# First norm, bias rows, cumulative-sum rows and the entry of the down stages: four edits to a two-block transformer kernel on one core

## The reference

```python
# first block
h = rms_norm(x, ln_mix_pre)
proj = h @ w_in                      # q, k, v, z, xbc, dt_raw
attn = moba_attention(q, k, v, rel_bias)   # one block of 256: causal, with a relative bias per head
ssm  = mamba2_mixer(z, xbc, dt_raw, ...)   # 16 heads, chunks of 128 tokens
#   a_cs = cumsum(dt * a);  seg = a_cs[l] - a_cs[s];  decay = exp(causal(seg))
#   y_diag = (C B^T * decay) @ (x * dt)
x = x + rms_norm(concat(attn, ssm) @ w_out, ln_mix_post)
h = rms_norm(x, ln_ffn_pre)
u = causal_conv(h @ w_ffn_up);  f = (gelu(gate) * up) @ w_ffn_down
x = x + rms_norm(f, ln_ffn_post)
# second block: rwkv7 in both directions + grouped attention, w_out2, and a
# product-key expert layer (top 16 of 128x128 experts in 8 heads), then a last norm
```

## Time and profile before

| | |
|---|---|
| median of 3 runs | 3450.74 us (3445.03 to 3453.64) |
| the profiled execution | 3449.55 us; span of its trace 3447.8 us |
| PE busy in the span | 3327.2 us (97%) |
| DVE, ACT, POOL busy | 2564.5 us (74%), 1609.3 us (47%), 131.9 us (4%) |
| w_in stage (chunks 0 to 44) | from 16 us to about 340 us |
| share of the DMA engines, 30 to 340 us | 0.47 |

### The profile page before, as it was taken

How to read it: one execution, slowest core, us unless ns; L and a number is a source line. 1 busy time by engine, 2 the same in 40 slices (tenths; PEclk the granted TensorE clock), 3 DMA queues, 4 the chain that set the end, 5 groups by cost and what they waited for, 6 DMA issues and landing times.

```text
span 3447.8 us, 68503 instructions
## 1 busy us (share of the span) xinstructions
PE 3327.2 (97%) x24846; PEld 2959.5 (86%) x24846; DVE 2564.5 (74%) x4463; ACT 1609.3 (47%) x2555; POOL 131.9 (4%) x143
## 2 busy tenths in 40 slices
PE   8999999999999999988888999999999999999998
PEld 6888878888888777777777899899999999999998
DVE  6766587776868788776665688877777887777776
ACT  5445554444444555543334522454544545454543
POOL 0000000000000000000000001100001010101000
PEclk9999999999999999999999999999999999999999
DMA  5534545555555544430002545688878788878764
GB/s 194 176 136 163 188 144 177 192 171 191 183 191 184 192 132 141 140 111 9 9 15 86 179 158 175 242 278 282 280 268 286 282 319 265 299 255 304 251 230 158
DMA packets 176239, 658.33 MB, mean 191 GB/s; under 512 B 20080, under 2 KB 28400, under 8 KB 167408
## 3 DMA queue, kind: packets, MB, share of 16 engines
q1 hardware_dynamic: 159744, 559.15, 48.1%
q0 software_dynamic: 16336, 97.03, 7.7%
HBM read 637.99 MB, written 17.04 MB: 190 GB/s over the span
## 4 chain that ended last, share of the span: by engine, by line
PE 82%; DVE 9%; DMA 3%; ACT 3%; issue 2%; ACTq 0%; DVEq 0%; SPq 0%
PE bank L609 47%; PE bank L611 23%; PE bank L1002 5%; DMA raw<-in_v_tab 3%; DVE w_lo L2113 2%; PE bank L1305 2%; DVE hot_row L3088 1%; ACT w_hi L1390 1%; DVE hot_col L3083 1%; DVE proj L2730 1%; PE bank L973 0%; DVE h_tok L3114 0%; PE bank L947 0%; PE bank L1013 0%; DMA gates<-g_stage 0%
## 5 line engine op out<-in xcount | busy, mean ns | idle before, releaser
L609 PE MATMUL bank<-h_two,w_hi 128*128 128x512 f32 (+1 forms) x5360 | 1821.9, 390 | 26.9 <-DVE w_lo L2113 19.2
L611 PE MATMUL bank<-h_two,w_lo 128*128 128x256 f32 (+1 forms) x5360 | 1466.8, 274 | 0.0
L2113 DVE TENSOR_TENSOR w_lo<-raw,w_hi 128x1024 fp32r<-128x1024 f32 (+1 forms) x1054 | 1228.5, 1184 | 232.8 <-ACT w_hi L1390 230.9
L1390 ACT ACTIVATE w_hi<-raw 128x1024 fp32r<-128x1024 f32 (+1 forms) x1054 | 1044.6, 1024 | 459.7 <-PE bank L611 239.9
L609 PEld LDWEIGHTS bank<-h_two,w_hi 128*128 128x128 f32 x5360 | 1006.7, 188 | 217.3 <-issue 19.6
L611 PEld LDWEIGHTS bank<-h_two,w_lo 128*128 128x128 f32 x5360 | 1016.6, 190 | 1.2 <-issue 1.0
L609 PE MATMUL bank<-p_two,w_hi 128*128 128x448 f32 x1792 | 569.9, 376 | 3.1 <-DVE acc L2154 2.4
L611 PE MATMUL bank<-p_two,w_lo 128*128 128x224 f32 x1792 | 475.9, 266 | 0.0
L609 PEld LDWEIGHTS bank<-p_two,w_hi 128*128 128x128 f32 x1792 | 336.2, 188 | 37.4 <-DVE w_lo L2113 6.3
L611 PEld LDWEIGHTS bank<-p_two,w_lo 128*128 128x128 f32 x1792 | 342.2, 191 | 0.0
L1399 ACT ACTIVATE stage<-bank 128x256 f32<-128x256 f32 (+1 forms) x242 | 89.2, 369 | 412.1 <-PE bank L611 412.0
(11 more groups left out here) (417 smaller groups left out, 3261.5 us busy)
## 6 DMA issues: line engine op xcount, KB each, us to landing
raw<-in_u_tab SPq DMA_DIRECT2D x256, 512.0 KB, 5.3
raw<-in_v_tab SPq DMA_DIRECT2D x256, 512.0 KB, 5.4
raw<-in_w_up SPq DMA_DIRECT2D x176, 512.0 KB, 4.2
raw<-in_w_in SPq DMA_DIRECT2D x174, 512.0 KB, 3.7
raw<-in_w_out SPq DMA_DIRECT2D x64, 512.0 KB, 4.1
raw<-in_w_down SPq DMA_DIRECT2D x64, 512.0 KB, 3.5
raw<-in_w_pq SPq DMA_DIRECT2D x32, 512.0 KB, 4.6
gates<-g_stage POOLq DMA_DIRECT2D x14, 896.0 KB, 6.4
```

Of the source, the lines that this page charges most:

```text
L609: first = nc.tensor.matmul(o[:, 0:2 * width].rearrange("p (a t) -> p a t", a=2), wh, pair[:, :, 0:width], start=(k == 0), stop=False)
L611: last = nc.tensor.matmul(o[:, width:2 * width], wl, pair[:, 0, 0:width], start=False, stop=(k == nk - 1))
L1390: nc.scalar.activation(w_hi[c % 2][:, at:end], raw[c % 2][:, at:end], ACT.Copy).then_inc(hi_done, 1)
L2113: nc.vector.tensor_tensor(w_lo[c % 2][:, at:end], raw[c % 2][:, at:end], w_hi[c % 2][:, at:end].bitcast(F32), ALU.subtract).then_inc(lo_do ...
```

## The change

Four edits:

- **First norm.** ACT squares all 16 tiles with no wait (into `quad` and two parts of `proj` not yet in use), DVE adds the four groups to one, and PE sums once, 4 matmuls after chunk 1, in place of 16 inside chunk 0. Chunks 0 and 1 are drained (copied and added) ahead of the reciprocal and scaled after it; chunks 2 and 3 wait for their bank's `added` only. Seven matmuls on x of 128x512 columns, whose result nobody reads, stand ahead of chunk 0 on PE.
- **Bias.** One product makes all 8 heads' rows (8x512), after chunk 2; ACT copies it once; POOL's queue stores each head's row 128 times from the one partition that holds it.
- **Cumulative sums.** PE makes 16x256 once, after chunk 5; DVE copies it out, ACT's queue stores it to DRAM, and POOL's queue loads it, four heads at a time, into all 128 partitions of `quad`. `segments(h)` reads `quad`. `acs_rows` is gone from PE.
- **Down stages.** The second half of the second w_down chunk is split over its 384 columns, not 1024, and on DVE its first half comes ahead of `conv`, its second ahead of `product`.

```diff
@@ PE
+            pe.wait_ge(s_x[0], 16)
+            keep_clocked(7, xT[:, 0, 0:P], xT[:, 0:2, :].rearrange("p a t -> p (a t)"))
             for n in range(IN1):
                 if n == 0:
-                    unscaled_chunk(0, "mix_pre", s_cst)
+                    chunk(0, 0, h_two, per_tile=first_groups)
+                elif n == 1:
+                    chunk(1, 0, h_two)
+                    pe.wait_ge(s_cst, 16)
+                    squares_sum("mix_pre")
                 else:
-                    chunk(n, 0, h_two)
-                if 2 <= n < 2 + HEADS1:
-                    toeplitz(n - 2)
+                    chunk(n, 0, h_two, bank_free=(added, n - 1) if n < 4 else None)
+                if n == 2:
+                    bias_rows()
...
-                if 0 <= n - SSM_AT < SSM_H:
-                    acs_rows(n - SSM_AT)
...
+            def squares_sum(name):
                 pe.wait_ge(quad_ready, QR[name] + 3)
                 for k in range(4):
                     last = nc.tensor.matmul(bank[2][:, 0:T], ones, quad[0][:, k, :], start=(k == 0), stop=(k == 3))
                 last.then_inc(sq_summed, 4)
...
+            def bias_rows():
+                pe.wait_ge(relb_loaded, 16)
+                pe.wait_ge(pool_set, 2)
+                nc.tensor.matmul(bank[3][0:HEADS1, :], relb[0:33, :], cst[0:33, C_BUCKET:C_BUCKET + 512],
+                                 start=True, stop=True).then_inc(toep_done, 1)
...
@@ dt_sums, PE
+                rows = bank[5][0:SSM_H, T:2 * T]
+                nc.tensor.matmul(rows, dta[:, 0:16], causal, start=True, stop=False)
+                nc.tensor.matmul(rows[:, P:T], dta[:, 16:32], causal[:, 0:P], start=False, stop=True
+                                 ).then_inc(acs_done, 1)
@@ ACT
             split(1, 0)
-            square("mix_pre", 2)
-            square("mix_pre", 3)
+            for g, dst in enumerate((quad[0], quad[1], proj[:, 0:4, :], proj[:, 4:8, :])):
+                nc.scalar.activation(dst[:], xT[:, 4 * g:4 * g + 4, :], ACT.Square).then_inc(sq_ready, 1)
+            nc.scalar.preload_act_table(ACT.Sqrt)
+            split_part(2, 0, 0)
+            copy(0, 0, dt_T[:])
+            split_part(2, 0, 1)
+            to_stage(1, 0, S_XBC, 0)
...
-                split(N_FFN + 2 * FQT + 1, it0)
+                split(N_FFN + 2 * FQT + 1, it0, FQT)
@@ POOL's queue
+            pool.wait_ge(toep_copied, 1)
             for h in range(HEADS1):
-                pool.wait_ge(toep_copied, h + 1)
-                pool.dma_start(toep_d[h:h + 1, 0:P * 512].rearrange("a (p n) -> (a p) n", n=512), toep[h % 2][:]
+                pool.dma_start(toep_d[h:h + 1, 0:P * 512].rearrange("a (p n) -> a p n", n=512),
+                               bias_row[h:h + 1, :].unsqueeze(1).to_broadcast([1, P, 512])
                                ).then_inc(toep_out[h % 2], 16)
...
+            pool.wait_ge(acs_stored, 32)
+            for q in range(4):
+                if q >= 2:
+                    pool.wait_ge(seg_done, 4 * q - 4)
+                pool.dma_start(quad[q % 2][:].rearrange("p h t -> p (h t)"),
+                               acs_d[0:1, 4 * T * q:4 * T * (q + 1)].to_broadcast([P, 4 * T])
+                               ).then_inc(acs_loaded[q % 2], 16)
@@ DVE
-            rstd(RS["mix_pre"])
+            for g, of in enumerate((quad[1], proj[:, 0:4, :], proj[:, 4:8, :])):
+                squares_added("mix_pre", g, of)
+            first_two("mix_pre", 0, 1, (dt_T[:], stage[0][:]), 1)
...
+                lower_part(c + 1, it0, 0)
                 conv(FQT - 1)
-                lower_part(c + 1, it0, 0)
+                lower_part(c + 1, it0, 1, FQT)
                 product(FQT - 1)
-                lower_part(c + 1, it0, 1)
```

More of the change, by code:

```diff
@@ L280, in build @@
         dts = sb("dts", [P, 9, TT * SSM_H], at=part)
-        toep = [sb(f"toep{j}", [P, 512], at=part) for j in range(2)]
+        bias_row = sb("bias_row", [P, 512], at=part)
+        acs_row = sb("acs_row", [P, 512], at=part)
         relb = sb("relb", [64, HEADS1], at=part)
@@ L658, in _, with keep_clocked @@
             BY_GROUPS = tuple((j, 4 * g, 4 * g + 4) for g in range(4) for j in range(2))
-            def keep_clocked(n):
+            def keep_clocked(n, lhs=ones, rhs=cst[:, 0:512]):
                 for _ in range(n):
-                    nc.tensor.matmul(bank[7][:], ones, cst[:, 0:512], start=True, stop=True)
+                    nc.tensor.matmul(bank[7][:], lhs, rhs, start=True, stop=True)
             def normed_by(first):
@@ L707, in total_sum @@
                 last.then_inc(sq_summed, 1)
[L709 to L716, removed]
+            def bias_rows():
[3 more added lines that the diff above has]
+                                 start=True, stop=True).then_inc(toep_done, 1)
             def scores(h):
                 if h == 0:
-                    pe.wait_ge(toep_copied, HEADS1)
+                    pe.wait_ge(toep_copied, 1)
                 else:
@@ L772, in dt_sums @@
                 nc.tensor.matmul(bank[5][:, 48:64], causal[:, P:T], dta[:, 0:16], start=True, stop=False)
-                nc.tensor.matmul(bank[5][:, 48:64], causal[:, 0:P], dta[:, 16:32], start=False,
-                                 stop=True).then_inc(acs_done, 1)
+                nc.tensor.matmul(bank[5][:, 48:64], causal[:, 0:P], dta[:, 16:32], start=False, stop=True)
+                rows = bank[5][0:SSM_H, T:2 * T]
+                nc.tensor.matmul(rows, dta[:, 0:16], causal, start=True, stop=False)
+                nc.tensor.matmul(rows[:, P:T], dta[:, 16:32], causal[:, 0:P], start=False, stop=True
+                                 ).then_inc(acs_done, 1)
             def x_turned(u):
@@ L792, in cb_products @@
                                  start=True, stop=True).then_inc(cb_done, 1)
[L794 to L804, removed]
             def ssm_outputs(h):
@@ L1476, in _, with bias_rows_copy @@
             split(0, 0)
-            square("mix_pre", 0)
-            square("mix_pre", 1)
             split(1, 0)
-            square("mix_pre", 2)
-            square("mix_pre", 3)
+            for g, dst in enumerate((quad[0], quad[1], proj[:, 0:4, :], proj[:, 4:8, :])):
[5 more added lines that the diff above has]
+            to_stage(1, 0, S_XBC, 0)
             act.wait_ge(pool_set, 1)
             rms(RS["mix_pre"], SUM["mix_pre"] + 4)
[L1484 to L1488, removed]
+            def bias_rows_copy():
+                act.wait_ge(toep_done, 1)
+                nc.scalar.activation(bias_row[0:HEADS1, :], bank[3][0:HEADS1, :], ACT.Copy).then_inc(toep_copied, 1)
             def exps(h):
@@ L1545, in _ @@
             for n in range(IN1):
-                if n == 0:
-                    copy(n, 0, dt_T[:])
-                elif n < 13:
+                if 1 < n < 13:
                     to_stage(n, 0, S_XBC + n - 1, 0)
-                else:
+                elif n >= 13:
                     copy(n, 0, proj[:, IN1_TILES[n], :])
@@ L2334, in segments @@
             def segments(h):
-                dve.wait_ge(acsb_done, h + 1)
+                if h % 4 == 0:
+                    dve.wait_ge(acs_loaded[h // 4 % 2], 16 * (HEADS1 // 2 + 1 + h // 8))
                 if h >= 2:
                     dve.wait_ge(mt_done, h - 1)
-                b = bank[5][:, T * (h % 2):T * (h % 2) + T]
+                b = quad[h // 4 % 2][:, h % 4, :]
                 nc.vector.tensor_scalar(seg[h % 2][:, 0:T], b, acs[:, h:h + 1], 0.0, ALU.subtract, ALU.min)
@@ L2379, in _ @@
             for n in range(IN1):
-                add_scaled(n, n + 1, dt_T[:] if n == 0 else stage[(n - 1) % 2][:] if n < 13 else proj[:, IN1_TILES[n], :],
-                           n + 1)
+                if n > 1:
+                    add_scaled(n, n + 1, stage[(n - 1) % 2][:] if n < 13 else proj[:, IN1_TILES[n], :], n + 1)
                 if 0 <= n - SSM_AT - 1 < SSM_H:
@@ L2399, in _ @@
                     dt_op(nc.vector.tensor_copy(acs, bank[5][:, 32:64]))
+                    nc.vector.tensor_copy(acs_row[0:SSM_H, 0:T], bank[5][0:SSM_H, T:2 * T]).then_inc(acs_rows, 1)
                 if n in X_AT:
```

38 lines of the change are left out of this document (25 added, 13 removed).

## The result

| | before | after |
|---|---|---|
| median | 3447.98 us (4 runs, 3445.03 to 3453.64) | 3477.53 us (4 runs, 3470.24 to 3487.4) |
| profiled execution, span | 3449.55, 3447.8 | 3470.24, 3468.5 |

The changed kernel takes 1.0085 of the time before, 95% interval [1.0069, 1.0101]: slower, where I forecast 3419.6 us. The time lies outside the range, and on the other side of no change.

The account below looks back on a forecast made before the run. The prediction took PE to be the bound. Its terms, 8.0 + 8.0 + 11.0 - 0.75 + 3.6 = 29.9 us, off the profiled 3449.55 gave 3419.6 us, range 3413 to 3426; 3412 to 3440 was to hold 0.8.

Parts of the forecast that it names:

- What bounds the kernel: From 30 to 340 us PE waits for nobody, so removed matmul time is saved if DVE, ACT and loads keep up.
- First norm, 8.0 us: At PE's start: chunk 3 would begin at 36.4 us and not at 44.43, a gain of 8.0 us.
- the 1.4 us of idleness should cost nothing: Ahead of chunk 0: idle matmuls end at 14.7 us, and PE's wait until 16.16 would not slow the next matmuls.
- Bias, 8.0 us on PE: After chunk 2: one of eight products stays on PE, saving 7 x 1.15 = 8.0 us.
- Cumulative sums, 10.25 us: On PE: sixteen heads' sums removed save 11.0 us; one added pair after chunk 5 costs 0.75 us.
- Down stages, 3.6 us: At four down-stage entries: the 1.49 us `w_lo` wait goes, the drain wait lengthens, 4 x 0.9 = 3.6 us won.
- The sum of the four, 29.9 us: Whole kernel: first norm, bias, cumulative sums and down stages together save 29.9 us.
- the unknown cost: Bias stores repeating one partition's row: taken between 3.6 and 9.3 us each, costed at nothing.
- The upper bound of 128 us: One bias store's time from one partition if time went with partitions, from 256 KB out of 32 landing in 4.0 us.
- the threshold: Bias stores may take 9.3 us each, ending at 112.9 us, for the bias to land in time at 121.4.
- The prediction's own sign of being wrong: PE waiting for weights between 38 and 115 us, with landing times well over 4 us.
- The stores hold up the weights: Rival, chance 0.12: slow bias stores delay weight loads on the same 16 engines; at 9.3 us each, 51 us lost, 3471.

Follow-up runs that it names:

- experiment 5: Changed kernel with two bias stores from one partition, six from DRAM: 3426.13 us, 0.9926; its distances run from chunk 3's first matmul to the feed-forward stage's first.
- experiment 2: Changed kernel with the eight bias rows stored to DRAM once and the 128-fold stores reading them there: 3417.35 us, 0.9914 of the kernel before.

## Why the prediction was wrong, point by point

- **What bounds the kernel: right.** The sums gave their time back in full, the norm 7.2 us of 8.0, the bias part all of it where its stores are cheap (each below), and in the two kernels with cheap stores PE waits for weights for 0 (rows from DRAM) and 1.1 us (sixteen partitions) between 30 and 450 us.
- **First norm, 8.0 us: right in size.** Alone 10.3, interval 5.9 to 15.2. By the trace chunk 3 began at 37.25 and not at the forecast 36.4: 7.2 us won against the earlier trace rows (44.43). What failed is one step, "the 1.4 us of idleness should cost nothing": the seven ended at 13.7 and not 14.7, PE idled for 2.04 us, and six pairs at 0.63 instead of 0.35 cost 1.7 us. Chunk 0 itself began 0.4 us early and the rest came out 0.4 us short, which hides half of that. With the clock kept chunk 3 began at 35.94, 20.05 us after chunk 0, where the forecast had 20.2. The steps on DVE came within 1.2 us: additions from 20.62, reciprocal at 31.19, and no wait at chunks 2 and 3.
- **Bias, 8.0 us on PE: right.** The kernel with sixteen partitions is 6.2 us faster than the one with the bias part undone (3415.41, 3421.63), from runs whose own spread is 4 to 5 us. By the distances of experiment 5 it is 8.35 us with rows from DRAM: 383.74 with the part undone (419.50 less 35.76), 375.39 without slow stores.
- **Cumulative sums, 10.25 us: right.** Alone 10.3, interval 5.9 to 14.8.
- **Down stages, 3.6 us: a little high.** 2.7 by its waits. The lengthened wait for the drain, which I had at 1.25 to 1.35, is 1.5 to 1.6. My list of what the profile would show had 1.5 to 1.9 for it, which does not fit a gain of 0.9 an entry; the sum used the smaller figure.
- **The sum of the four, 29.9 us: right where the stores are cheap.** Sixteen partitions: 0.991, that is 31 us, interval 24 to 37.
- **The step that failed** is the unknown cost: "I take a value between 3.6 and 9.3, nearer to the row with the same bytes and destination, and cost it at nothing." Measured: 9.5 us a store, and a loss of 60.5 us where the sum has nothing. The row I leaned on had 128 source partitions; I matched bytes and destination, and the property that decides was the source. The upper bound of 128 us was too far away to warn, so I should have taken the middle of a wide range as likely, not its lower end. By the Trainium skill, "SBUF — State Buffer", section on Door 1, I had an estimate of 9.5 us for a store. The trace agrees: 76.3 us for eight.
- **And the threshold was worked out for the wrong path.** I asked only how late the bias may land (9.3 us a store), and by that 9.5 us would have cost 2. The bias was never the problem: its loads were issued at 115.54, 2.6 us after the 112.9 that I had allowed, and from 120 to 450 us PE waits for nobody. What decided was what else stood behind the same sixteen DMA engines. Where the stores may end by 112.9 without harm to their reader, the loaded weights covered only some 17 us from their start at 39.24. The prediction's own sign of being wrong, a wait for weights between 38 and 115 us, is what the trace shows.
- **The rival was right, its chance wrong.** "The stores hold up the weights", 0.12, priced at 51 us lost and 3471 us for 9.3 us a store. PE's waits are 56.2 us; behind each of the two long ones PE ran seven or eight pairs at the low level, (0.63 - 0.35) x 15 = 4.2 us. Together 60.4 us, and the loss against stores from DRAM is 60.5 by the traces. Its model, one half chunk per store, gives 53 us at 9.5 us a store (8 x 9.5 - 23) and was too mild: from 40 to 112 us SP's queue moved 1.89 MB, 3.6 halves, 20 us each, twice a store. What I held against it, that eight stores at 3.6 us went by with PE busy, was evidence only for stores that are not slow at their source.
- The Trainium skill, "DMA: Bandwidth & Descriptors", section on back-pressure in remote DMA, says that stalled writes also stall the other queues of the DMA engine they come from. It says so of writes, in transfers between cores; these runs show the like for slow reads out of one SBUF partition. That it is by the same mechanism no run here shows: I see that the sixteen engines count as occupied and that the other queue's packets come rarely, not what they wait for inside.

Left open: whether different rows out of one partition are as slow as one row read 128 times, whether fewer partitions than sixteen would do (nothing between 1 and 16 was measured), and whether the loss would vanish if the stores went over fewer of the sixteen DMA engines; none of it was tried.

## What to carry to other kernels

A DMA that repeats a row can take work off PE and still lose, if it reads it out of one SBUF partition: before moving a broadcast from PE to DMA, spread the row over some sixteen partitions or write it to DRAM once and read it there (2.3 and 1.9 us per 256 KB here, one behind the other, against 9.5). When a new transfer has no row in the trace, find the nearest row by its source, destination and shape separately, and ask not only how late its own reader gets it but who shares its engines, how long their buffers last, and what a us of occupation costs from there. A DMA share near 1 at a quarter of the usual GB/s (1.01 at 56 here) was the mark of this fault; a share near 1 alone is not (0.91 at 294 GB/s in experiment 2, with PE always busy).

## What the runs showed of the hardware

- 256 KB out of one SBUF partition took 9.5 us from GpSimd's queue and 9.6 from ACT's: 262,144 bytes in 9.54 us (76.3/8) are 27.5 GB/s. The same rows read 128 times each from DRAM took 1.9 us a store: the repeated reads of one DRAM row were not slow. Out of sixteen partitions, 8 times each, it took 2.3 us.
- A queue with slow reads held the other queue of the same engines to a seventh of its packets (848 to 123 in 18 us), at a DMA share of 1.01.
- Idleness of 1.86 to 2.04 us behind seven matmuls was followed by matmuls at the 1.2 GHz level in four traces; idleness of 0.73 to 1.54 us was not in four others, nor was the 1.49 us of the earlier trace rows.
- Eight issues of these stores held ACT for 55.6 us, where POOL had issued the same eight in 4.32 us. What held ACT no run shows.
